# Choosing the experts of three token tiles during the output projection, and splitting the first expert's row products by token tile

## The reference, cut to what matters

```python
x = x + g1 * (y @ w_out[layer])
h2 = rms_norm(x, norm2_g[layer]) * (1 + sc2) + sh2
scores = jax.nn.sigmoid(jnp.dot(h.astype(F32), router_w.astype(F32)))
biased = scores + router_b.astype(F32)
grp = biased.reshape(h.shape[0], N_EXPERT_GROUPS, EXPERTS_PER_GROUP)
grp_score = jnp.sum(lax.top_k(grp, TOP_K)[0], axis=-1)
best = jnp.argmax(grp_score, axis=-1)
masked = jnp.where(expert_group[None, :] == best[:, None], biased, -jnp.inf)
_, idx = lax.top_k(masked, TOP_K)
for e in range(N_EXPERTS):
    he = jax.nn.silu(h @ w1[e]) * (h @ w3[e])
    y = y + gates[:, e:e + 1] * (he @ w2[e]).astype(F32)
return rms_norm(x + g2 * y, final_g)
```

## Time and profile before

| | us |
|---|---|
| median of 3 runs | 594.47 (594.21 to 595.01) |
| the profiled execution | 592.3 |
| its span | 590.5 |
| TensorE busy | 550.4 (93%) |
| VectorE busy | 447.2 (76%) |
| ScalarE busy | 322.7 (55%) |
| GpSimd busy | 148.4 (25%) |
| bytes moved, mean rate | 171.81 MB, 291 GB/s |

### The profile page before, as it was taken

One profiled execution on the slowest core, in us unless ns is written; L12 is line 12 of the kernel. 1 busy time (PEld: TensorE's weight loads), 2 busy tenths in 40 slices (PEclk: granted clock), 3 DMA queues, 4 the chain that ended last, 5 costly groups with the idle time before them and its releaser, 6 DMA issues.

```text
span 590.5 us, 7645 instructions
## 1 busy us (share of the span) xinstructions
PE 550.4 (93%) x2733; PEld 418.2 (71%) x2733; DVE 447.2 (76%) x577; ACT 322.7 (55%) x401; POOL 148.4 (25%) x137
## 2 busy tenths in 40 slices
PE   1789999999998999977998999999999999999995
PEld 1446865677676788747587888888888888778772
DVE  1357699436585635346979999999999999999868
ACT  4631133445336822244646876676876677866624
POOL 5000923322311500012243311333212333210060
PEclk9899999999999999997999999999999999999998
DMA  8999995867225700166879999999999999999665
GB/s 303 389 373 318 379 379 188 276 206 268 73 71 194 263 8 39 69 236 229 288 268 386 387 391 391 393 392 393 390 389 391 389 383 387 383 378 362 206 216 211
DMA packets 89178, 171.81 MB, mean 291 GB/s; under 512 B 5427, under 2 KB 18935, under 8 KB 89153
## 3 DMA queue, kind: packets, MB, share of 16 engines
q1 hardware_dynamic: 83010, 153.34, 72.6%
q10 hardware_dynamic: 2768, 9.97, 4.2%
q0 software_dynamic: 3376, 8.18, 3.9%
HBM read 158.06 MB, written 17.32 MB: 297 GB/s over the span
## 4 chain that ended last, share of the span: by engine, by line
PE 83%; DMA 6%; DVE 5%; ACT 3%; issue 2%; SPq 1%; DVEq 0%; ACTq 0%
PE psum L887 6%; PE psum L1220 4%; PE psum L1222 4%; PE psum L1221 4%; PE psum L1247 4%; PE psum L1249 4%; PE psum L1248 4%; PE psum L1232 4%; PE psum L1230 4%; PE psum L1231 4%; PE psum L895 4%; DMA w<-in_moe_w 3%; PE psum L932 3%; DMA ada<-in_ada_w 3%; PE psum L934 3%; PE psum L933 3%
## 5 line engine op out<-in xcount | busy, mean ns | idle before, releaser
L2143 DVE TENSOR_TENSOR w_lo<-w,w_hi 128x2048 fp32r<-128x2048 f32 x32 | 72.9, 2281 | 2.4 <-ACT w_hi L1634 2.4
L2132 DVE TENSOR_TENSOR w_lo<-w,w_hi 128x1024 fp32r<-128x1024 f32 (+2 forms) x30 | 68.8, 2293 | 0.0
L1625 ACT CAST w_hi<-w 128x2048 fp32r<-128x2048 f32 x30 | 57.2, 1910 | 15.6 <-PE psum L1232 10.9
L1634 ACT CAST w_hi<-w 128x2048 fp32r<-128x2048 f32 x32 | 60.1, 1916 | 5.3 <-PE psum L1249 3.0
L2126 DVE TENSOR_TENSOR w_lo<-w,w_hi_a 128x2048 fp32r<-128x2048 f32 (+1 forms) x30 | 51.5, 1755 | 2.9 <-ACT w_hi_a L1621 2.1
L760 POOL COPY idx<-idx 128x1 int32 (+1 forms) x14 | 13.6, 971 | 147.6 <-PE psum L1194 147.5
L1247 PE MATMUL psum<-w_hi,heT_hi 128*128 128x512 f32 x120 | 49.5, 412 | 0.8 <-DVE w_lo L2143 0.8
L1807 DVE SCALAR_TENSOR_TENSOR rows<-ada,cc,rows 128x512 f32<-128x512 f32 x48 | 41.8, 874 | 9.1 <-DMA ada<-in_ada_w 7.6
L1249 PE MATMUL psum<-w_hi,heT_lo 128*128 128x512 f32 x120 | 47.0, 392 | 0.0
L1221 PE MATMUL psum<-w_lo,xgT_hi 128*128 128x512 f32 x120 | 46.8, 390 | 0.0
L1230 PE MATMUL psum<-w_hi,xgT_hi 128*128 128x512 f32 x120 | 46.7, 389 | 0.0
(11 more groups left out here) (350 smaller groups left out, 1252.2 us busy)
## 6 DMA issues: line engine op xcount, KB each, us to landing
w<-in_moe_w SPq DMA_DIRECT2D x32, 2048.0 KB, 15.0
w<-in_moe_w SPq DMA_DIRECT2D x32, 1024.0 KB, 14.2
ada<-in_ada_w SPq DMA_DIRECT2D x12, 2048.0 KB, 18.2
win<-in_w_in SPq DMA_DIRECT2D x8, 1024.0 KB, 14.4
expert_rows<-ysb ACTq DMA_DIRECT2D x15, 512.0 KB, 6.3
expert_rows<-zero SPq DMA_DIRECT2D x1, 5120.0 KB, 21.2
wout<-in_w_out SPq DMA_DIRECT2D x4, 1024.0 KB, 4.9
x<-in_x SPq DMA_DIRECT2D x2, 1024.0 KB, 9.9
```

The lines of the kernel that those rows point to most:

```text
L1634: act.copy(w2_hi[:, :, hs], w2_sb[b][:, :, hs]).then_inc(w2_hi_ok[half], 1)
L2132: v.tensor_tensor(w3_lo[b][:, ks, :], w3_sb[b][:, ks, :], w3_hi[:, ks, :], ALU.subtract).then_inc(w3_lo_ok, n)
L2143: v.tensor_tensor(w2_lo[b][:, :, hs], w2_sb[b][:, :, hs], w2_hi[:, :, hs], ALU.subtract).then_inc(w2_lo_ok[half], 1)
```

## The change

**TensorE.** `project(6)` is cut after 3 depth steps, `project(7)` after 2 and 5, and `turn_x1(2)` with `logits(1)`, `logits(2)` and the first half of `turn_x1(3)` stand in the cuts. Ranks of tiles 0 to 2 are counted into bank 6 as soon as their experts are chosen. `keep_busy` is gone. `first_rows` is split by token tile: for k = 0 to 5 the parts of tiles 0 to 2 come first, in banks 0, 1, 4, 5, 2, 3; after k = 4 all ranks are counted into bank 7; the parts of tile 3 follow. `plain1` starts when five of the eight k are copied out; `rows_in` stands between the halves of `plain3`, and `overflow_index` behind it.

```diff
+            project(6, 0, 3)
             turn_x1(2)
             logits(1)
+            project(6, 3)
             router(2)
+            project(7, 0, 2)
             logits(2)
+            project(7, 2, 5)
+            turn_x1(3, (0,))
+            project(7, 5)
+            router(3, 0, 4)
+            turn_x1(3, (1,))
+            router(3, 4)
             logits(3)
...
+            pe.wait_ge(sel_ok, 1)
+            for t in range(NT - 1):
+                m = ranks(bank[6], t)
+            m.then_inc(rank_ok, 1)
 
             pe.wait_ge(x1_ok, 2 * NT)
             row_sum(6)
             row_sum(7)
...
-            keep_busy(3)
...
+            for k in range(6):
                 if k >= 4:
+                    pe.wait_ge(rows_act, k + 3)
+                first_rows(k, range(NT - 1))
+                if k == 4:
+                    pe.wait_ge(prob_ok, 2)
+                    pe.wait_ge(sel_ok, 2)
+                    for t in range(NT):
+                        ranks(bank[7], t)
...
+            for k in range(6):
+                first_rows(k, range(NT - 1, NT)).then_inc(x0_ps, 1)
+            for k in (6, 7):
+                pe.wait_ge(x0_ok, k - 5)
+                first_rows(k, range(NT)).then_inc(x0_ps, 1)
             pe.wait_ge(hot_ok, 1)
...
             plain1()
+            plain3(0, 4)
+            rows_in(1, 1, 0)
+            plain3(4, KD)
             overflow_index()
-            rows_in(1, 1, 0)
-            plain3()
```

```diff
+            chances(0, NT - 1, 1)
             squares2(6)
+            x1T_copy(3, (0,))
+            act.activation(st2[:, 1, 5:6], eps[:], ACT.Sqrt)
             squares2(7)
+            x1T_copy(3, (1,))
...
-            high_w1(1, 1, 0)
             act.wait_ge(rwq_ok, 1)
             for k in range(KD):
+                if k == 1:
+                    store_h2(3)
+                if k == 6:
+                    act.wait_ge(w1_in[1], 16)
+                    high_w1_part(1, 0)
+                    high_w1_part(1, 1)
```

```diff
+            link(mixed(1))
+            residual(6)
+            mixed(2).then_inc(mix_ok, 1)
             v.wait_ge(prob_ok, 1)
...
+            early_choice()
+            residual(7)
+            early_second()
+            norm2(TL)
+            early_chosen()
+            norm2_root(TL)
...
+            mixed(TL).then_inc(mix_ok, 1)
+            v.wait_ge(rank_ok, 1)
...
+            for t in range(NT - 1):
+                first_matrix(t)
+            v.wait_ge(prob_ok, 2)
+            late_choice()
...
+            v.wait_ge(sel_ok, 2)
...
             v.tensor_scalar(hot_base[:, :, 0, :], ohf, tok[:, 0:1], None, ALU.mult)
+            v.wait_ge(rank_ok, 2)
...
+            first_matrix(TL)
+            v.wait_ge(scale_ok, 3)
+            v.tensor_tensor(h2[:, 1, :], h2[:, 1, :], rows[:, SH2, :], ALU.add).then_inc(h2_ok, 1)
...
+            low_rows(1)
             low_w2(0, 0, 0)
+            gated(0)
             index(NE, NB, 2)
+            v.tensor_copy(gslot[:], bank[6][:, 2 * OVER:2 * OVER + NB]).then_inc(idx_ok, 1)
             overflow_list()
...
             low_w2(0, 0, 1)
+            low_hidden(0, 0)
             low_w3(1, 1, 0, 2)
-            low_hidden(0, 0)
             low_w3(1, 1, 2, 2)
             v.wait_ge(rows_act, 8)
             expert_rows(0, 0, 0, 0)
+            combine_terms()
```

More of the change, by code:

```diff
@@ L1062, in project_first, with project @@
                 m.then_inc(wo_ok, 1)
-            def project(n):
+            def project(n, first=0, stop=KD):
                 t, half = n // 2, n % 2
-                if 1 <= n < 4:
+                if first == 0 and 1 <= n < 4:
                     pe.wait_ge(rows_act, n + 1)
-                if n >= 4:
+                if first == 0 and n >= 4:
                     pe.wait_ge(x1_ok, n - 3)
-                for k in range(KD):
+                for k in range(first, stop):
                     tc, cc_ = slice(t * P, (t + 1) * P), slice(half * 512, (half + 1) * 512)
@@ L1075, in project, with turn_x1 @@
                                   stop=(k == KD - 1))
-                m.then_inc(wo_ok, 1)
-            def turn_x1(t):
-                for g in range(2):
+                if stop == KD:
+                    m.then_inc(wo_ok, 1)
+            def turn_x1(t, halves=(0, 1)):
+                for g in halves:
                     pe.wait_ge(x1_ok, 2 * t + g + 1)
@@ L1090, in quarter_bank, with router @@
                 return bank[6][:, P:P + 2] if t < 0 else bank[6][:, 0:P]
-            def router(t):
-                for k in range(KD):
+            def router(t, first=0, stop=KD):
+                for k in range(first, stop):
                     if k % 4 == 0 and t >= 0:
@@ L1125, in _, with ranks @@
             router(1)
-            project(6)
+            project(6, 0, 3)
             turn_x1(2)
             logits(1)
+            project(6, 3)
             router(2)
-            project(7)
-            turn_x1(3)
+            project(7, 0, 2)
             logits(2)
-            router(3)
-            logits(3)
+            project(7, 2, 5)
[4 more added lines that the diff above has]
+            router(3, 4)
+            logits(3)
+            def ranks(to, t):
+                for i in range(t + 1):
+                    m = pe.matmul(to[:, t * NE:(t + 1) * NE], tri[:] if i == t else ones_b[:],
+                                  sel[:, i, :], start=(i == 0), stop=(i == t))
+                return m
+            pe.wait_ge(sel_ok, 1)
+            for t in range(NT - 1):
+                m = ranks(bank[6], t)
+            m.then_inc(rank_ok, 1)
             pe.wait_ge(x1_ok, 2 * NT)
@@ L1152, in _ @@
[L1152 to L1157, removed]
-                if k >= 4:
[L1160 to L1164, removed]
@@ L2022, in _ @@
[L2022 to L2031, removed]
@@ L2069, in _ @@
             ins.then_inc(hot_ok, 1)
+            pick(expert[:], eno[:].unsqueeze(1).unsqueeze(1).to_broadcast(E2))
             def index(b0, b1, n):
```

180 lines of the change are left out of this document (109 added, 71 removed).

## The result

The changed kernel takes 588.13 us (median of 4 runs, 586.42 to 588.51), the kernel before 594.38 (4 runs beside it): 6.25 us less, a ratio of 0.9888 with a 95% interval of 0.9872 to 0.9904. That is faster by five times what a measurement of this kernel can tell from no change. The profiled execution takes 588.02 us with a span of 586.3.

What follows compares the result with a forecast made beforehand. It took the loop's start, set by a chain of waits through VectorE's choice and TensorE, as the bound. The profiled 592.3 us less 6.7 is 585.6; with the median 2.2 above, it said 587.7, range 585.0 to 591.5.

Steps and rivals of the forecast that it cites:

- Projection and early choice: Before the expert loop: residual(7) 0.5 us later, ending at 256.7; early choice on VectorE takes 2.8 us, from 251.2.
- The cover: On VectorE, early choice ends at 254.9, 0.4 us ahead of residual(7), so it does not delay it.
- the second rival: First chances later than 251.6, by a drain or otherwise, so residual(7) waits: all 1.0 us later, 588.8; chance 0.1.
- Late choice: On VectorE after the sigmoid: 20 instructions of 16 columns take 3.9 us, from 260.75 to 264.65.
- First rows and the clock: On TensorE: 30 early matmuls take 3.45 us at the full clock; `plain1` starts at 270.0, 9.2 us earlier.
- The gather: Behind the h2 store of 7.0 us: SyncE's w3 load 5.5 us later, at 279.8, just ahead of `rows_in` at 280.3.
- VectorE's line: From 270.2 to the end of `gated(1)`: 33.5 us of work and 2.2 of waits, 305.9 against 312.53.
- TensorE's 9.2 us: On TensorE alone, `plain1` starts 9.2 us earlier and would keep that to `hidden1`; VectorE limits the shift to 6.7.
- I take its shift as the shift of the end: The shift of `hidden_turned(1)`, the last stop before the expert loop, 6.7 us, is the shift of the kernel's end.
- agreeing: SyncE's weight queue: 6 MB from 279.8 are through by 297, against 304, so the stream starts some 7 us earlier.
- The fourth rival: The weight stream sets the end and starts when the gather lands; at 281.6 the gain is lost: 594; chance 0.05.
- The first rival: TensorE's clock falls around row sums and 30 early matmuls; ranks 3.6 us later, gain 3.1, 591.4; chance 0.14.

Runs made afterwards that it cites:

- e1_busy8: The kernel before with eight filler products instead of three on TensorE, from the row sums until the experts are chosen: 594.69 us, ratio 0.9997.
- e4_no_split: The changed kernel with TensorE's first rows not split by token tile, waiting for all chosen experts: 592.48 us, ratio 0.9958 to the kernel before.
- e5_gate_first: The changed kernel with gated(1) ahead of the three low_w1 of expert 2 on VectorE: 586.86 us, ratio 0.9867 to the kernel before.
- e2_fill: The changed kernel with two filler products ahead of hidden_turned(1) on TensorE: 587.37 us, ratio 0.9882 to the kernel before.
- e12_gate_again: The same program as e5_gate_first, run again beside the changed kernel on the same chip: 586.99 us, ratio 0.9873 to the kernel before.
- e10_gate_light: e5_gate_first with the gather fetching 64 of 1024 columns from expert 2 on, not the reference's rows: 584.60 us, ratio 0.9833 to the kernel before.
- e7_w3_free: The changed kernel with w3 of expert 1 issued without waiting for the gathered rows: 588.99 us, ratio 0.9902 to the kernel before.
- e9_light: The changed kernel with the gather fetching 64 of 1024 columns from expert 2 on, not the reference's rows: 586.41 us, ratio 0.9851 to the kernel before.
- e11_after_again: The changed kernel again, unchanged, beside e12_gate_again on the same chip: 587.67 us, ratio 0.9887 to the kernel before.
- e3_old_tail: The changed kernel with the old order behind plain1 on TensorE and VectorE: 598.29 us, ratio 1.0042 to the kernel before.
- e6_gate_fill: e5_gate_first with the two filler products of e2_fill: 586.87 us, ratio 0.9872 to the kernel before.

## Why the prediction was right

587.7 was predicted, 588.13 measured; a gain of 6.7, and 6.25 was measured. It was right in the place and, up to `hidden_turned(1)`, in the mechanism. That the number is this close is luck: two of its terms were off, by 1.5 and 1.6 us in opposite directions, and cancelled. (Its sum is also loose by 0.1 twice: 312.5 less 305.9 is 6.6, and 585.6 and 2.2 are 587.8.)

- **Projection and early choice.** The 0.5 us of delay was right: residual(7) starts at +13.99, predicted 255.3, which is +14.1. The cover held with 0.67 us to spare (0.4 predicted). The drain of the second rival does not show here: the square root starts 0.01 us behind its load. By the drain of 1.38 us that the Trainium skill gives (ScalarE: Activation LUTs, What ACT_TABLE_LOAD costs) it would have started at 258.7; the trace has 257.31.
- **Late choice.** Predicted 3.9 us, measured 4.0. I had 0.21 us for each instruction; those that compare with a value of each partition (L2081, L2088, L2092) take some 0.27 from start to start, the first ones less than 0.21.
- **First rows and the clock.** 3.45 predicted for 30 products, 3.51 measured. Predicted `plain1` at 270.0, +28.8; measured +28.20. e1_busy8 and e4_no_split show the clock as part of it: 1.6 us.
- **The gather.** Store 7.3 (7.0 predicted), then 4.4 us to SyncE's load instead of 5.5. `rows_in` did not wait.
- **VectorE's line, the first term that was off.** Predicted `hidden_turned(1)` at 305.9, which is +64.7; measured +63.19. The line starts 0.5 us earlier, and the wait of 1.1 for the high part of `he` was 0.26, since w3's cast began at +46.2, 1.1 us earlier than predicted (288.5, which is +47.3). That TensorE's 9.2 us would be cut to VectorE's was right: `hidden1` is 9.1 earlier, `hidden_turned(1)` 8.1, and e5_gate_first removed just that wait.
- **"I take its shift as the shift of the end", the second.** This step of the prediction failed. 1.6 of the 8.1 us are given back: the clock falls behind the 2.19 us gap at `hidden_turned(1)`, where the gap of 1.53 in the kernel before did not do it, and where that is mended (e2_fill, e12_gate_again) about 0.9 us more go in late steps, because the weights are late. The prediction had the stream as "agreeing" with 7 us; at its start it did agree (w2 of expert 2 is issued at +54.2 instead of +63.0), but it left out that a backlog grows through the loop. e10_gate_light against e12_gate_again shows that this sets the late steps. The fourth rival, by which the stream starts when the gather lands, had the right bound in the wrong size: the gain is not lost, but what is added to it comes through in part only.
- **The first rival** was real too. In e7_w3_free and e9_light the clock is 0.50 at 262 to 264:

```profile
262.00:264.00 2.00, 2.00 (x5) 0.96 (x4) 1.71 (x11) 1.31 (x3) 0.00 (x0) 0.50 1.04 395
```

  The price is 1.3 us at `plain1` (+29.5 instead of +28.2), not 3.6, since only a part of this work ran at the low clock: in e9_light the row sums take 3.64 us and the 30 early products 3.51 as at the full clock, in e7_w3_free 3.23 and 3.96. So the same program pays it in some executions, in two of the eleven that have it.

What stays open: whether an earlier h2 store, which needs its addition ahead of the late choice, would bring the gather, hot_mod and w3 earlier for more than it costs. It was not tried. Nor is it known why hot_mod takes 6.7 us in one execution and 9.1 in another.

## What to carry to other kernels

When work moves ahead of a loop that is itself near two limits, follow the shift to the end of the loop and not to its start: here engines won 8.1 us and 6.5 arrived. Of the 1.5 to 1.6 us more that e2_fill and e12_gate_again have at expert 3, 0.6 and 0.7 arrived; with bytes left out (e10_gate_light against e11_after_again) 1.5 at expert 3 became 2.9 at the end, since the late steps went too. The time that the same load takes to land, early and late in the loop, is the sign to look for. Here splitting a product by what is known early paid twice, by the overlap and by an engine that has no gap in which its clock falls. And a reordering that looks like tidying can be the condition of the gain: with the old order behind it this change made the kernel slower than before.

## What the runs showed of the hardware that I had not expected

- A gap on TensorE ahead of `hidden_turned(1)` was followed by the clock of 0.50 in the changed kernel (2.19 us), e11_after_again (2.18), e9_light (2.36) and e7_w3_free (2.08), but not in e4_no_split (2.08), nor in the kernel before (1.53). After the lull of 258 to 261, the same program kept 1.00 in nine executions and fell to 0.50 in two.
- Eight GpSimd instructions that make hot_mod took 4.79 us in the kernel before, 4.77 in e1_busy8 and 4.78 in e4_no_split, 6.7 to 6.9 in most of the others, and 9.10 and 9.09 in e3_old_tail and e6_gate_fill. In the three short ones the gather ahead of them waited for `idx` and its instruction took 2.27 us, in the others it waited for the h2 store and took 1.15 or 1.16. The cause was not found.
- An h2 store of 512 KB took 7.0 to 8.2 us in all these executions, though it was issued with 12 us of backlog in the kernel before and with 8 in the changed one.
